# End of the expert stage: the last but one tile's down product ahead of the last tile's up products, and the rows asked back behind the last matrix

## The reference, cut to what matters

```python
gate = p_g * top_p / jnp.sum(top_p, axis=-1, keepdims=True)   # two experts of 32 for each token
expert = grp * EXP_PER_GROUP + top_i
...
def run_block(args):
    tok, e = args
    xb = x_pad[tok]
    return (jax.nn.silu(xb @ w1[e]) * (xb @ w3[e])) @ w2[e]
...
y = yb.reshape(P, D) * slot_g[:, None]
return jax.ops.segment_sum(y, slot_t, num_segments=T + 1)[:T]
...
h = h + m_lat[5] * f.reshape(B, S, D)
```

## Time and profile before

| | |
|---|---|
| median of three runs | 2500.44 us (2494.41 to 2502.44) |
| span of the profiled execution, first to last instruction | 2494.6 us (no time of its own is listed beside it) |
| TensorE matmul busy | 2372.1 us, 95% |
| TensorE weight load busy | 1058.1 us, 42% |
| VectorE busy | 1143.0 us, 46% |
| ScalarE busy | 361.5 us, 14% |
| GpSimd busy | 294.1 us, 12% |
| DMA | 239 GB/s over the span, about 400 GB/s in the expert stages |
| mean granted clock of TensorE | 0.985 of full speed |

### The profile page before, as it was taken

How to read it: one execution, slowest core, us unless ns; L and a number is a source line. 1 busy time by engine, 2 the same in 40 slices (tenths; PEclk the granted TensorE clock), 3 DMA queues, 4 the chain that set the end, 5 groups by cost and what they waited for, 6 DMA issues and landing times. The chain is left out here.

```text
span 2494.6 us, 33367 instructions
## 1 busy us (share of the span) xinstructions
PE 2372.1 (95%) x14149; PEld 1058.1 (42%) x14150; DVE 1143.0 (46%) x2405; ACT 361.5 (14%) x645; POOL 294.1 (12%) x313
## 2 busy tenths in 40 slices
PE   4999999989999999999999899999999999999997
PEld 3545444544555523333233344444555333334433
DVE  1788377767945423322222544434455223322226
ACT  2310233331012200000000240000121000000002
POOL 2000000001000222122220000000002122221200
PEclk9999999999999999999999999999999999999999
DMA  9577100020170599999999611112106999999994
GB/s 307 200 251 275 34 26 26 17 110 34 68 286 34 213 357 402 402 404 413 388 409 410 240 34 51 34 51 85 76 29 254 378 406 402 414 402 414 406 379 202
DMA packets 140530, 581.41 MB, mean 233 GB/s; under 512 B 16756, under 2 KB 41640, under 8 KB 87768
## 3 DMA queue, kind: packets, MB, share of 16 engines
q1 hardware_dynamic: 120648, 534.87, 55.1%
q0 software_dynamic: 19648, 44.09, 4.8%
q10 hardware_dynamic: 80, 0.26, 0.0%
HBM read 550.74 MB, written 44.32 MB: 239 GB/s over the span
## 5 line engine op out<-in xcount | busy, mean ns | idle before, releaser
L1709 PE MATMUL ps<-arena 128*32 128x512 f32 x6144 | 678.9, 595 | 16.8 <-DMA arena<-in_ex_w_dram 16.8
L1709 PEld LDWEIGHTS ps<-arena 128*32 128x32 f32 x6144 | 207.2, 110 | 440.7 <-issue 423.7
L1744 PE MATMUL ps<-arena 128*32 128x512 f32 x3072 | 344.2, 598 | 11.2 <-DMA arena<-in_ex_w_dram 11.1
L1869 PE MATMUL ps<-arena 128*128 128x512 f32 x616 | 264.5, 592 | 0.0
L2497 DVE TENSOR_TENSOR arena<-arena,ps 128x512 f32<-128x512 f32 x48 | 52.3, 1090 | 456.2 <-PE ps L1709 456.2
L1589 PE MATMUL ps<-arena 128*128 128x512 f32 x512 | 229.4, 598 | 1.6 <-DVE arena L2273 1.6
L1744 PEld LDWEIGHTS ps<-arena 128*32 128x32 f32 x3072 | 119.1, 111 | 226.2 <-issue 207.5
L822 POOL DMA_INDIRECT arena<-normed_rows,arena x184 | 185.7, 1009 | 111.6 <-issue 52.5
L2542 DVE TENSOR_TENSOR arena<-ps,gates 128x512 f32<-128x512 f32 x96 | 61.8, 686 | 257.4 <-PE ps L1744 257.4
L1869 PEld LDWEIGHTS ps<-arena 128*128 128x128 f32 x616 | 117.0, 190 | 147.3 <-issue 147.3
L1402 PE MATMUL ps<-arena 128*128 128x512 f32 x384 | 167.3, 593 | 0.7 <-issue 0.7
(11 more groups left out here) (325 smaller groups left out, 2297.0 us busy)
## 6 DMA issues: line engine op xcount, KB each, us to landing
arena<-in_ex_w_dram SPq DMA_DIRECT2D x384, 1024.0 KB, 10.5
arena<-in_mod_w_dram SPq DMA_DIRECT2D x24, 2048.0 KB, 8.7
arena<-expert_rows SPq DMA_DIRECT2D x16, 1024.0 KB, 7.7
arena<-in_od_w_in_dram SPq DMA_DIRECT2D x12, 1024.0 KB, 5.4
arena<-in_x_dram SPq DMA_DIRECT2D x2, 4096.0 KB, 15.4
expert_rows<-gates SPq DMA_DIRECT2D x8, 1024.0 KB, 22.4
normed_rows<-arena POOLq DMA_DIRECT2D x16, 512.0 KB, 2.9
arena<-in_ev_w_in_dram SPq DMA_DIRECT2D x3, 2048.0 KB, 13.1
```

The lines of the kernel that those rows point to most:

```text
L1709: ins = nc.tensor.matmul(bank(2 + m)[c:c + n], x[:, j, c:c + n], w_slot(e % 2, m, KC, FE)[:, j], start=j == 0, stop=j == KC - 1)
L1744: ins = nc.tensor.matmul(bank(5 + half)[c:c + n], HT[:, j * P + c:j * P + c + n], w_slot(e % 2, 2, FC, D)[:, j, half * 512:(half + 1) * 51 ...
L1869: ins = nc.tensor.matmul(bank(4 * (g % 2) + b), x[:, j], y[:, j], start=first and j == 0, stop=j == 3, skip_group_check=True)
```

## The change

Three engines get another order at the end of the expert stage, in both layers. TensorE: down(22) goes ahead of ups(23), with 3 spare matmuls ahead of it, and the 12 spare matmuls ahead of down(23) become 6 ahead of turn(23) and 3 behind it. SP: both halves of expert 31's w2 go ahead of all rows; the first half now waits for half of down(22) by a lower count of `half_mm`. VectorE: rows(22), add 0 and add 1 go ahead of hidden(23), and rows(23) goes ahead of add 5, 6 and 7.

```diff
@@ -588,24 +588,19 @@
-                    if p == NP - 1:
-                        for b in range(2):
-                            sp.wait_ge(y_out[b], 16 * NL * (l + 1))
-                        for i in range(2):
-                            rows_back(2 * l, i)
-                        sp.wait_ge(gate_mm, n0 + NP)
-                        for i in range(2, 4):
-                            rows_back(2 * l, i)
                     if freed_down:
-                        sp.wait_ge(half_mm, halves_before(l, p) + 3)
+                        sp.wait_ge(half_mm, halves_before(l, p) + 3 if p < NP - 1 else 3 * NP * l + 3 * (NP - 1))
                         for e in freed_down:
                             weights(e, 2, (0,))
-                        if p == NP - 1:
-                            rows_back(2 * l, 4)
                         sp.wait_ge(y_mm, n0 + p)
                         for e in freed_down:
                             weights(e, 2, (1,))
-                for i in range(5, TT):
+                for b in range(2):
+                    sp.wait_ge(y_out[b], 16 * NL * (l + 1))
+                for i in range(2):
+                    rows_back(2 * l, i)
+                sp.wait_ge(gate_mm, n0 + NP)
+                for i in range(2, TT):
                     rows_back(2 * l, i)
@@ -1757,14 +1752,19 @@
-                for p in range(NP):
+                for p in range(NP - 1):
                     pass_ups(p)
                     if p:
                         pass_down(p - 1)
                     else:
                         pe.wait_ge(tab_ready, l + 1)
                     turn_hidden(p)
-                spare(12, 0)
+                spare(3, 0)
+                pass_down(NP - 2)
+                pass_ups(NP - 1)
+                spare(6, 0)
+                turn_hidden(NP - 1)
+                spare(3, 0)
                 pass_down(NP - 1)
@@ -2563,21 +2563,22 @@
                 for p in range(NP):
                     if p + 1 < NP:
                         x_cols(p + 1)
+                    if p == NP - 1:
+                        pass_rows(p - 1)
+                        add_rows(2 * l, 0, GM[:, 0])
+                        add_rows(2 * l, 1, GM[:, 0])
                     pass_hidden(p)
-                    if p == NP - 1:
-                        for i in range(1, 4):
-                            add_rows(2 * l, i, GM[:, 0])
-                    if p:
+                    if p and p < NP - 1:
                         pass_rows(p - 1)
                     if 4 <= p < 4 + TT:
                         late_hot(p - 4)
                     if 3 <= p < 3 + TT:
                         gated_hot(p - 3)
-                    if p == NP - 2:
-                        add_rows(2 * l, 0, GM[:, 0])
-                for i in range(4, TT):
+                for i in range(2, 5):
                     add_rows(2 * l, i, GM[:, 0])
                 pass_rows(NP - 1)
+                for i in range(5, TT):
+                    add_rows(2 * l, i, GM[:, 0])
```

## The result

The changed kernel takes **2522.24 us** (2518.55 to 2528.49, four runs), the kernel before 2501.20 us in its four (2494.41 to 2502.44). The ratio is 1.0094 with a 95% interval of 1.0072 to 1.0117: 0.9% slower, inside the range, and close to the 2522.5 us of the prediction.

A forecast was written before the change was run, and what follows sets the result against it. The additions and the row blocks they wait for were taken to bound the late sums. Layer shifts of 10.9 and 9.9 us plus 1.6 us for the cold clock gave 22.4 us: 2522.5 us, 0.9% slower, range 2505 to 2533.

The forecast's parts named there:

- What bounds the kernel now: End of the expert stage: late sums wait for VectorE's additions and their row blocks; TensorE could gain nothing alone.
- Term 1: Down(22), ahead of ups(23), waits 5.3 and 4.7 us for expert 30's w2 half, then takes 9.0 us from a slow start.
- Term 2: From ups(23)'s end, block 2, additions and rows(23) take 23.4 and 24.3 us to the late sums: +10.9 and +9.9 us.
- Term 3: Layer 1's late sums start at half clock after TensorE's idle stretch: +1.6 us, and 0 in layer 0.
- Hidden(23) covered: Add 0 and 1 ahead of hidden(23) cost nothing: add 1 ends 1 us ahead of the end of ups(23).
- the first: Rival at down(22): its matrix is there in time, so no wait; 2509 us, 13%.
- The last matrix: Rival at the late sums: they start behind down(23) and the additions keep up; faster, 2488.6 us, 4%.
- Blocks one at a time: Rival at VectorE's row blocks: blocks 5, 6 and 7 each come late, 4.8 us more per layer; 2532 us, 10%.
- The ends: Rival for the whole: the ends hide each other, within 0.3%, 2500 us, 3%.

The follow-up runs named there:

- e5: Kernel before, with the third row buffer moved off tile 23's input and blocks 0 to 3 asked for without the wait for ups(23): 2500.12 us.
- e3: Changed kernel, with the third row buffer moved off tile 23's input, so block 2 doesn't wait for ups(23), and rows(23) last on VectorE: 2514.65 us.
- e6: Changed kernel, third buffer moved, three row blocks asked for before expert 31's w2, ups(23) split around down(22), VectorE reordered: 2509.47 us.
- e1: Changed kernel, with the load of the second half of expert 30's w2 left out in both layers: 2514.44 us.
- e2: Changed kernel, with 15 instead of 3 spare matmuls ahead of down(22): 2518.05 us.
- e7: Changed kernel, with 25 spare matmuls behind down(23), ahead of the late sums: 2520.09 us.
- e4: Changed kernel, third buffer moved, blocks 0 to 2 asked for ahead of expert 31's w2, add 0 to 4 ahead of hidden(23): 2503.86 us.
- e9: Kernel before, with only TensorE's order changed and the count of half_mm it needs: 2526.57 us.

## Why the prediction was right, point by point

- **What bounds the kernel now:** right. The additions and the rows they need set the end. In the kernel before, an earlier request for block 2 brought nothing (e5). In the changed kernel it did, 2.5 and 4.7 us (e3), while in e6 a down(23) that ended 6 us earlier than in the kernel before brought nothing.
- **Term 1, the wait:** foretold 5.3 and 4.7 us, measured 5.91 and 5.66; the half landed 7.5 us behind its request in layer 1, not 7.1. The price of 4.4 us by the formula of the Trainium skill, "DMA: Bandwidth & Descriptors", Anatomy of one DMA, didn't hold for this transfer in a filled queue, as rows 5 had said; that section gives the formula for transfers issued by GpSimd, and this one comes from SP. Down(22) itself: 9.0 foretold, 9.01 and 9.48 measured. e1 took away the slow start and 4.3 and 3.8 us of the wait, e2 the slow start alone, and each gave back about that (12.9 and 5.6 us in distance for 12.4 and 4.3).
- **Ups(23):** foretold 30.1 us behind turn(22) in layer 1 and 29.5 in layer 0, measured 30.5 and 30.8.
- **Term 2, what hangs on it:** foretold 23.4 and 24.3 us, measured 25.5 and 23.9. The excess in layer 1 is block 7 (8.2 us on the way, 1.64 us of wait) and a little of block 5. I had kept such a delay for block 5 and asked nothing of block 7. In e1, e2 and e7 the same stretch took 23.2 to 24.5 us, so the term is sound to 2 us. The 0.6 us kept in layer 0 for a longer way of block 2 wasn't needed: it took 4.85 us there.
- **Term 3, the cold late sums:** 1.6 foretold, 1.7 in the tail, and e7 takes it away.
- **Hidden(23) covered:** right, by less than foretold: add 1 ended 0.5 us ahead of the end of ups(23) in layer 1, and level with it in layer 0. In e1 and e4, where ups(23) came earlier or more additions stood ahead of hidden(23), the cover was gone in layer 0 (waits of 1.31 and 3.78 us).
- **The sum:** 10.9 + 9.9 + 1.6 = 22.4 foretold; by the distances 13.4 + 10.8 + 1.7 = 25.9. That the median lies within 1 us of the forecast is partly luck: executions differ by some 8 us ahead of the change alone. Three slips in the working have no weight: 2500.44 + 22.4 is 2522.8 and not 2522.5; with its 3 spares down(22) starts 12.4 us sooner, not 14; and rows 9 show the half clock for layer 1's down(23) only (in layer 0 the trace has 0.50 in 1401.1 to 1404.4 us).
- **The rivals:** the wait at down(22) was there, so the first fell. The last matrix decided nowhere in the changed kernel, so the one on the fast side fell; in e4 rows(23) waits for down(23) in both layers, and even there it is no gain. Blocks one at a time came true for block 7 alone, by 1.6 us instead of 4.8, and in layer 1 only. The ends didn't hide each other: the distances grew in both layers.

Open: why down(22) has its matrix and starts 6.3 us behind turn(22) in both layers of e9, and only after 7.5 to 8.2 in the other kernels that put it there, and why block 3 took 13.7 us in e4's layer 0. GpSimd's small router loads are issued shortly before, and e4's queues move 264 GB/s in 1389 to 1393 us against 424 GB/s in 2439 to 2443 us of its layer 1, but no run took those loads away.

## What to carry to other kernels

Moving a product ahead of another to have its result sooner also moves the moment at which its operands must be there; the time between the request of the last operand and the new start is the first thing to read. Where an engine works through a queue in order, count what stands behind the instruction that waits: how many additions stood behind hidden(23) decided most variants here, and in e6 TensorE's gain of 6 us vanished into idle time. To judge an edit of some microseconds in a program of 2500, measure between two marks in the trace on either side of it, since the medians hide it, and profile a kernel more than once: between two executions of the same instructions these distances differed by up to 2.5 us.

## What the runs showed of the hardware that I had not expected

The same instructions ahead of the change took up to 8 us more or less from one execution to the next (turn(22) of layer 0 at 1364.3 to 1372.3 us). The cold start of down(22) varied too: 8.4 to 10.0 us behind waits of 4.3 to 6.3 us, without the longest wait giving the longest product. How long TensorE had been idle didn't settle the clock of layer 1's late sums either: they started at full clock behind 2.95 us in the kernel before and 2.68 in e4, but in e5 at 0.51 for the first 3.3 us behind only 2.29 us, with a tail of 37.5 instead of 35.9 us. Why isn't known.
